# DeltaNet key, value, q and z projections of the second block from high and low parts of h, with beta and dt on four column strips behind the keys

## The reference, cut to what matters

```python
h  = modulate_2(x, norm1_g, sh1, sc1)       # rmsnorm(x) * gain * (1 + scale) + shift
hc = modulate_2(xc, norm1_g, csh1, csc1)    # the same for the context
qkv, z, ba, sc_p, fn_u = split_cols(h @ w_in, IN_SIZES)   # q 512, k 512, v 512, z 512, ba 16, ...
...
qkv = silu(conv_fn(p_qkv, conv_w))          # three taps along the tokens, centred
beta = sigmoid(ba[..., :8])                 # two directions, four heads
g = -exp(a_log) * softplus(ba[..., 8:] + dt_bias)
```

## Time and profile before

| | us |
|---|---|
| three timed runs | 1872.82, 1873.57, 1874.22 (median 1873.57) |
| the profiled execution, its own time | 1871.45 |
| the profiled execution, its span | 1869.6 |
| PE busy | 1780.8 (95% of the span) |
| DVE busy | 913.7 (49%) |
| ACT busy | 614.3 (33%) |
| POOL busy | 125.4 (7%) |
| mean granted TensorE clock | 0.985 |

### The profile page before, as it was taken

One profiled execution on the slowest core, in us unless ns is written; L12 is line 12 of the kernel. 1 busy time (PEld: TensorE's weight loads), 2 busy tenths in 40 slices (PEclk: granted clock), 3 DMA queues, 4 the chain that ended last, 5 costly groups with the idle time before them and its releaser, 6 DMA issues.

```text
span 1869.6 us, 25422 instructions
## 1 busy us (share of the span) xinstructions
PE 1780.8 (95%) x10086; PEld 1337.9 (72%) x10086; DVE 913.7 (49%) x1704; ACT 614.3 (33%) x1155; POOL 125.4 (7%) x138
## 2 busy tenths in 40 slices
PE   6998899999999999898999999999899899999998
PEld 2443445478888887453679999648579799889997
DVE  2133764263434344345736665344468854445554
ACT  3112554142323232133635444302320044034433
POOL 1001000100000001033000000100115000000000
PEclk9999999999999999998999999899999999999999
DMA  9223774322222223244044443313230334344442
GB/s 388 78 90 146 292 278 186 117 104 95 90 91 90 90 91 144 103 156 162 19 156 157 181 181 137 135 61 125 85 135 1 111 132 165 135 150 168 165 155 85
DMA packets 20886, 253.89 MB, mean 136 GB/s; under 512 B 2208, under 2 KB 4512, under 8 KB 5024
## 3 DMA queue, kind: packets, MB, share of 16 engines
q1 hardware_dynamic: 17712, 242.44, 34.2%
q10 hardware_dynamic: 3056, 9.82, 1.4%
HBM read 251.20 MB, written 1.05 MB: 135 GB/s over the span
## 4 chain that ended last, share of the span: by engine, by line
PE 83%; DVE 8%; ACT 3%; DMA 3%; issue 2%; POOL 1%; DVEq 0%; POOLq 0%; SPq 0%; ACTq 0%
PE bank L498 26%; PE bank L524 13%; PE bank L525 13%; PE bank L526 13%; PE bank L924 4%; PE bank L586 3%; PE bank L661 3%; PE bank L684 2%; PE bank L669 2%; DVE w_lo L1582 1%; DMA weights<-in_ada 1%; ACT w_hi L1187 1%; POOL root L2034 1%; ACT slab L1127 1%; DMA weights<-in_even_in 1%
## 5 line engine op out<-in xcount | busy, mean ns | idle before, releaser
L498 PE MATMUL bank<-slab,weights 128*128 128x256 f32 (+2 forms) x1456 | 445.2, 464 | 3.0 <-DVEq L1691 1.2
L498 PEld LDWEIGHTS bank<-slab,weights 128*128 128x128 f32 (+1 forms) x1456 | 272.8, 189 | 169.7 <-issue 134.2
L1582 DVE TENSOR_TENSOR w_lo<-weights,w_hi 128x1024 fp32r<-128x1024 f32 (+1 forms) x220 | 264.4, 1211 | 93.6 <-ACT w_hi L1187 92.7
L1187 ACT ACTIVATE w_hi<-weights 128x1024 fp32r<-128x1024 f32 (+1 forms) x220 | 228.4, 1046 | 215.9 <-PE bank L526 209.6
L524 PE MATMUL bank<-h_hi,w_hi 128*128 128x256 f32 (+1 forms) x864 | 273.9, 317 | 8.5 <-DVE w_lo L1582 5.9
L525 PE MATMUL bank<-h_lo,w_hi 128*128 128x256 f32 (+1 forms) x864 | 273.4, 316 | 0.0
L526 PE MATMUL bank<-h_hi,w_lo 128*128 128x256 f32 (+1 forms) x864 | 272.0, 315 | 0.0
L524 PEld LDWEIGHTS bank<-h_hi,w_hi 128*128 128x128 f32 x864 | 162.9, 189 | 24.9 <-issue 11.4
L525 PE MATMUL bank<-mlp_hidden_lo,w_hi 128*128 128x512 f32 (+1 forms) x512 | 174.4, 341 | 0.0
L524 PE MATMUL bank<-mlp_hidden_hi,w_hi 128*128 128x512 f32 (+1 forms) x512 | 173.3, 338 | 0.6 <-DVE w_lo L1582 0.6
L526 PE MATMUL bank<-mlp_hidden_hi,w_lo 128*128 128x512 f32 (+1 forms) x512 | 172.7, 337 | 0.0
(11 more groups left out here) (209 smaller groups left out, 2305.2 us busy)
## 6 DMA issues: line engine op xcount, KB each, us to landing
weights<-in_ada SPq DMA_DIRECT2D x36, 2048.0 KB, 7.6
weights<-in_mlp_up SPq DMA_DIRECT2D x16, 2048.0 KB, 8.4
weights<-in_mlp_down SPq DMA_DIRECT2D x16, 2048.0 KB, 8.4
weights<-in_ffn_in SPq DMA_DIRECT2D x11, 2048.0 KB, 7.5
weights<-in_in SPq DMA_DIRECT2D x8, 2048.0 KB, 8.5
weights<-in_gate SPq DMA_DIRECT2D x6, 2048.0 KB, 7.6
weights<-in_ffn_out SPq DMA_DIRECT2D x8, 1408.0 KB, 6.0
weights<-in_even_in SPq DMA_DIRECT2D x4, 2048.0 KB, 13.2
```

Of the source, the lines that this page charges most:

```text
L498: last = mm(b[rows, 0:width], lhsT(k), rhs(k), start=k == 0, stop=k == kc - 1)
L1187: A(split_part(w_hi, q), raw_part(q), ACT.Copy).then_inc(sem("w_hi_ready"), 1)
L1582: V.tensor_tensor(split_part(w_lo, q), raw_part(q), split_part(w_hi, q).bitcast(F32), ALU.subtract)\
```

## The change

Keys, values, q and z become `split_linear` layers. Norm 2's second half is written anew: DVE's 16 products go into h, ACT writes their sum with the shift as fp32r into `mix_hi` (16 instructions), DVE writes the low part `mix_lo` (16 instructions, between its products), and ACT then also adds the shift to h in place (16 instructions), since beta and dt, the branches and the gates still read h. PE is released chunk by chunk by `mix2_lo`. ACT and DVE split the first three weight parts ahead of the norm's root.

Beta and dt come behind the four key groups: the 16 weight columns are padded to 32, they are the stationary operand, the 512 tokens move, and the chunks k go to the column strips k % 4, all in one bank. ACT copies the bank to `ba_row`, and behind the first value group four small products add the strips and turn them tokens-first; one DVE copy then takes the place of four. DVE's gate arithmetic stands ahead of its step for v1 and v3, ACT's Sigmoid, Exp and Ln ahead of the Silu of v2.

The splitting of the weights is spread over the groups: ACT splits the high part of group i + 2 ahead of its Silu of group i, DVE the low part of group i + 1 ahead of its wait for group i. The arrays of the layer are placed anew so that `mix_hi` and `mix_lo` fit.

```diff
+            split_linear("in2", [1], tag=lambda m: ("k", m), lead=True, idle=(12, 4),
+                         before=lambda k, m: pe.wait_ge(sem("mix2_lo"), k + 1) if m == 0 else None, **mix_part(TOK))
             w = take_block("in2_ba", 0)
-            for t in range(4):
-                product(("ba", t), DC, lambda k: h[:, k, t * P:(t + 1) * P], lambda k: w[:, k, :], width=16,
-                        before=h_ready("mix2") if t == 0 else None, idle=12 if t == 0 else 0)
-            release_block(("ba", 3))
+            b = open_group(("ba", "strips"))
+            for k in range(DC):
+                pe.wait_ge(sem("mix2_h"), k + 1)
+                strip = slice(k % 4 * STRIP, (k % 4 + 1) * STRIP)
+                ins = mm(b[strip, :], w[:, k, :], h[:, k, :], start=k < 4, stop=k >= 4)
+            close(ins, ("ba", "strips"))
+            release_block(("ba", "strips"))
-            linear("in2", lambda k: h[:, k, :], TOK, tag="k", blocks=[1])
-            linear("in2", lambda k: h[:, k, :], TOK, tag="v", blocks=[2])
-            linear("in2", lambda k: h[:, k, 0:LAT], LAT, tag="q", blocks=[0])
-            linear("in2", lambda k: h[:, k, 0:LAT], LAT, tag="z", blocks=[3])
+            split_linear("in2", [2], tag=lambda m: ("v", m), after=lambda m: gates_tokens_first() if m == 0 else None,
+                         **mix_part(TOK))
+            split_linear("in2", [0], tag=lambda m: ("q", m), **mix_part(LAT))
+            split_linear("in2", [3], tag=lambda m: ("z", m), **mix_part(LAT))
...
+            def gates_tokens_first():
+                b = open_group(("ba", "tokens"))
+                drained(pe, ("ba", "strips"))
+                for t in range(4):
+                    ins = mm(b[:, t * 16:(t + 1) * 16], ba_row[:, t * P:(t + 1) * P], fold[:, 0:16], start=True, stop=True)
+                close(ins, ("ba", "tokens"))
... # scalar engine
-            norm("mix2", TOK, mix2_ready, (2, 0))
+            norm("mix2", TOK, mix2_ready, None, late=PARTS)
+            for c in range(DC):
+                for s in range(SIDES):
+                    act.wait_ge(sem("mix2_m"), c * SIDES + s + 1)
+                    A(mix_hi[:, c, cols], h[:, c, cols], ACT.Identity, bias=mod[2][:, c, s:s + 1])\
+                        .then_inc(sem("mix2_hi"), 1)
+            for c in range(DC):
+                act.wait_ge(sem("mix2_lo"), c + 1)
+                for s in range(SIDES):
+                    ins = A(h[:, c, cols], h[:, c, cols], ACT.Identity, bias=mod[2][:, c, s:s + 1])
+                ins.then_inc(sem("mix2_h"), 1)
+            for i in range(16):
+                split_until(min(parts_before("in2"), PART_END[(name, i % 4)] + PARTS))
+                if i == 4:
+                    copy_out(("ba", "strips"), ba_row)
+                if i == 6:
+                    act.wait_ge(sem("ba_dt"), 1)
+                    ...
... # vector engine
+            split_until(split[0] + PARTS)
             norm_root("mix2", TOK)
-            norm_scale("mix2", TOK, 2, 0)
+            for c in range(DC + 1):
+                if c < DC:
+                    for s in range(SIDES):
+                        V.scalar_tensor_tensor(out=h[:, c, cols], in0=x[:, c, cols], scalar=gains[2][:, c, s:s + 1],
+                                               in1=root[:, 0, cols], op0=ALU.mult, op1=ALU.mult)\
+                            .then_inc(sem("mix2_m"), 1)
+                if c:
+                    for s in range(SIDES):
+                        dve.wait_ge(sem("mix2_hi"), (c - 1) * SIDES + s + 1)
+                        ins = V.scalar_tensor_tensor(out=mix_lo[:, c - 1, cols], in0=h[:, c - 1, cols],
+                                                     scalar=mod[2][:, c - 1, s:s + 1],
+                                                     in1=mix_hi[:, c - 1, cols].bitcast(F32),
+                                                     op0=ALU.add, op1=ALU.subtract)
+                    ins.then_inc(sem("mix2_lo"), 1)
             for i in range(12):
                 t = (name, i % 4)
+                split_until(PART_END[t] + PARTS - 1)
+                if i == 5:
+                    gate_sums()
+                if i == 7:
+                    gate_logs()
                 filled(dve, t)
                 ...
                 conv3(conv[:, i % 3, :], bank(t), taps[:, c + i % 4, :], width, scaled)
+            split_until(parts_before("in2"))
```

More of the change, by code:

```diff
@@ L203, in build @@
         ada_row = root[:, 1, :]
+        ba_row = root[:, 1, :]
         warm = sb("warm", 1)
@@ L512, in linear, with split_linear @@
                     release_block(t)
-            def split_linear(name, blocks, hi, lo, width, tag, before=None, lead=False, idle=(0, 0)):
+            def split_linear(name, blocks, hi, lo, width, tag, before=None, lead=False, after=None, idle=(0, 0)):
                 rows, cols, _ = WEIGHTS[name]
@@ L566, in split_linear @@
                         close(last, t)
+                        if after:
+                            after(m)
                         m += 1
@@ L1115, in norm @@
                     A(dst, x[:, c, 0:width], ACT.Square).then_inc(sem(f"{name}_sq"), 1)
+                split_until(split[0] + late)
                 t = (name, "ss")
@@ L1329, in _ @@
-            for i in range(12):
-                name, dst, width = (("k", kT, TOK), ("v", vT, TOK), ("q", qT, LAT))[i // 4]
-                act.wait_ge(sem("conv"), i + 1)
-                A(dst[:, i % 4, 0:width], conv[:, i % 3, 0:width], ACT.Silu).then_inc(sem(f"{name}_silu"), 1)
-            for i in range(4):
-                filled(act, ("z", i))
-                A(zs[:, i, :], bank(("z", i))[:, 0:LAT], ACT.Silu).then_inc(free(("z", i)), 1)
+            norm("mix2", TOK, mix2_ready, None, late=PARTS)
@@ new lines, in gate_sums @@
+            def gate_sums():
+                t = ("ba", "tokens")
+                filled(dve, t)
+                V.tensor_copy(gsum, bank(t)[:, 0:64].rearrange("p (t c) -> p t c", c=16)).then_inc(free(t), 1)
+                drained(dve, t)
+                for t in range(4):
+                    link(V.tensor_tensor(dtmp[:, 0, t, :], gsum[:, t, 8:16], par("dt_bias"), ALU.add))
+                link(V.tensor_scalar(dtmp[:, 2], dtmp[:, 0], -1.0, None, ALU.mult))
+                link(V.tensor_tensor(dtmp[:, 1], dtmp[:, 0], dtmp[:, 2], ALU.max))
+                V.tensor_scalar(dtmp[:, 0], dtmp[:, 0], 0.0, None, ALU.max).then_inc(sem("ba_dt"), 1)
@@ new lines, in gate_logs @@
+            def gate_logs():
+                dve.wait_ge(sem("ba_dt"), 1)
+                dve.wait_ge(sem("gate_parts"), 3)
+                link(V.tensor_tensor(dtmp[:, 0], dtmp[:, 0], dtmp[:, 2], ALU.add))
+                for t in range(4):
+                    link(V.scalar_tensor_tensor(out=gl[:, t, :], in0=dtmp[:, 0, t, :], scalar=-1.0,
+                                                in1=decay[:, 0:8], op0=ALU.mult, op1=ALU.mult))
+                V.engine_nop().then_inc(sem("g_ready"), 1)
```

73 lines of the change are left out of this document (37 added, 36 removed).

## The result

The kernel after takes 1853.29 us (median of 4 runs, 1850.75 to 1860.84) against 1873.89 us for the kernel before on the same chip (4 runs, 1872.82 to 1877.64): ratio 0.9893, 95% interval 0.9880 to 0.9907. The forecast was 1853.2 in a range of 1847 to 1861. The profiled execution took 1854.92 us, with a span of 1853.0.

What follows compares the result with a forecast made beforehand. PE was taken to bound the projections. Terms summed to 79.3 us, with the clock's 1.7 to 81.0 against 101.3, 20.3 less: median 1853.2 us from 1873.57, range 1847 to 1861 for 8 in 10.

Steps and rivals of the forecast that it cites:

- Groups: Sixteen key, value, q and z groups: 82.6 us before, 67.8 in three passes, 14.7 less; 512-wide groups 5.60, 256-wide 2.88.
- rival (c): Projections: three passes cost three quarters of four when fed without a break, 61.9 us for 67.8; 1847.3, chance 0.06.
- (a): DVE stays behind after the fourth-key-group wait; eight value and q groups cost 1.3 us more each; 1863.5, chance 0.15.
- (d): Slower: each value and q group's low part waits for the step of the group just closed; 1884, chance 0.04.
- 1.4 us of slack: Each value group: DVE has 4.2 us of work against PE's 5.60, so low parts stay ahead.
- Start and three key groups: Keys start 2.74 us behind DVE's first product, at 1185.97; first three key groups take 16.87, ending at 1202.84.
- The gap: Before the fourth key group PE waits 4.8 us for DVE's low part, made behind two steps; bounds 2.2 and 6.5.
- ACT is just as late: At the fourth key group: ACT's high part is ready at 1206.0, near DVE's low part with hand-over at 1207.6.
- The clock in the gap: PE idles about 2.9 us before the fourth key group, the clock falls, 1.7 us lost; bounds nothing and twice that.
- Strips and small products: Beta and dt: eight strip products 1.9 us, four small products 0.95, at most twice that; ACT's table loads covered.
- Passage to q: From values to q PE waits 1.7 us, then 0.4 twice, for DVE's steps and low parts: 2.5 us, bounds 0 and 5.
- Rival (e): Projections' gain given back: l2 stage or delta net waits for a weight block; nothing left, 1873, chance 0.03.

Runs made afterwards that it cites:

- the experiments at the fourth group and at q: Kernel after with the fourth key group's parts made earlier, 1849.24 us; that kernel with weight parts one group further ahead from the last value group on, 1846.28 us.

## Why the prediction was right

By its own steps, from DVE's first product on.

**Groups.** DVE's steps for the values:

```profile
1221.03 0.75 DVE L1825 TENSOR_SCALAR slab<-bank,params 128x512 f32<-128x512 f32 x1 [3.48 <-PE bank L529]
...
1227.54 0.75 DVE L1825 TENSOR_SCALAR slab<-bank,params 128x512 f32<-128x512 f32 x1 [0.75 <-PE bank L529]
...
1233.14 0.75 DVE L1825 TENSOR_SCALAR slab<-bank,params 128x512 f32<-128x512 f32 x1 [1.44 <-PE bank L529]
...
1238.74 0.75 DVE L1825 TENSOR_SCALAR slab<-bank,params 128x512 f32<-128x512 f32 x1 [0.53 <-PE bank L529]
```

They are 5.60 apart, 6.51 where the small products lie, so rival (c) falls here as in the rows of before, and DVE waits ahead of each, so rivals (a) and (d) fall too. The forecast's 1.4 us of slack is there ahead of the third value step (1.44); where the gates' small instructions stand, ahead of the second and the fourth, 0.75 and 0.53 are left. So (a) had a true ground that was too small to matter here.

**Start and three key groups.** The keys start 2.73 us behind DVE's product (forecast 2.74) and the three groups take 1184.57 to 1201.45, 16.88 (16.87). The parts split ahead of the root cost nothing that shows.

**The gap.** 1201.45 to 1206.03, 4.58 (4.8), ended by DVE's low part, in the order that the forecast had:

```profile
1198.86 0.75 DVE L1825 TENSOR_SCALAR slab<-bank,params 128x512 f32<-128x512 f32 x1 [3.27 <-PE bank L529]
...
1201.73 0.75 DVE L1825 TENSOR_SCALAR slab<-bank,params 128x512 f32<-128x512 f32 x1
...
1204.66 1.22 DVE L1621 TENSOR_TENSOR w_lo<-weights,w_hi 128x1024 fp32r<-128x1024 f32 x1
```

"ACT is just as late" was wrong; it had its high part 1.1 us before DVE took it up:

```profile
1200.73 1.28 ACT L1374 ACT_TABLE_LOAD   x1
1202.02 0.63 ACT L1374 ACTIVATE slab<-slab 128x512 f32<-128x512 f32 x1
1202.56 1.04 ACT L1209 ACTIVATE w_hi<-weights 128x1024 fp32r<-128x1024 f32 x1
```

The Silu starts 0.01 us behind the load, so no row has room for a second piece, and leaving it out was right. The drain of about 1.38 us that the Trainium skill (ScalarE: Activation LUTs, What ACT_TABLE_LOAD costs) adds to a load is not borne out here.

**The clock in the gap.** 3.4 us at 0.51, so 1.7 lost, as taken. That it fell here was not certain: behind the same gap it fell in three of five profiles. The forecast had "nothing" as its other bound.

**Strips and small products.** 1.92 and, by the second value step, 6.51 - 5.60 = 0.91 (1.9 and 0.95). The gates' table loads lay under a value group.

**Passage to q.** From the last value step, at 1238.74, to the turn of v 25.3 us for eight groups of 2.88: 2.3 lost, 1.5 of them in the one wait at the second q group (2.5).

**Sum.** 20.3 us less was forecast for the stage and 20.6 measured. The bounds of its terms, added up, give 1846.4 to 1860.1 and not the 1848 to 1858 that it states; the range of 1847 to 1861 covers all but 0.6 us of that.

Rival (e), the gain given back downstream, came true in part in the profiled run, 5.3 us, but not as it was put: no weight block was waited for. One of the prediction's own signs of being wrong, a longer stage from the l2 norms on, did appear (220.57 against 215.25). For an execution like the profiled one it forecast 1851.1, and the profiled run of after took 1854.92, 3.8 more. The prediction had no term for half clock that comes and goes from run to run, though it makes up most of the range that the runs span. That the median fell within 0.1 us of the forecast is partly luck for this reason.

What the prediction did not see, as it priced only the sum: that one half of the change, made first, is worth three times the other in the stage, 15.7 to 4.9. The passes' gross gain of 14.7 was right. The gap with its clock (6.3), the passage to q (2.3) and the later start (1.3) took 9.9 of it back, and the experiments at the fourth group and at q recovered 6.8 of that.

## What to carry to other kernels

Price the two halves of a change apart, also where they come together: here the cheap one, moving small products off the head of a stage and giving them 512 columns, carries three quarters of the stage's gain when made first, and its time alone can't be told from that of the whole change. A faster product hands the bound to whoever prepares its operands: look for the first group whose preparation stands behind a consumer's step in the same queue, and move it ahead. And before a few us are explained, take the half-clock time out of the runs: time x clock tells kernels apart that their times do not.

## What the runs showed of the hardware

Products 16 columns wide ran with TensorE at 1.2 GHz at two places of the program. Behind the keys the clock fell 2.9 us into them, at 1222.2, though PE had been busy since 1213.60, and stayed at 0.50 over the next 8.00 us. Ahead of the keys it fell while PE was still waiting for ACT's shifts (busy 2.08 of 4.10 us), and stayed low while the products ran without a break (0.63 on the mean of the gates, rows 2). Eight products on strips with 512 columns had no such stretch behind them in the kernel with the gates alone moved. Time lost to half clock is most of what one run of a kernel differs by from the next: 30 to 43 us of 1871 to 1885 in the kernel before. An idle time of 2.69 us behind dummies was followed by 3.4 us at half clock in three profiles of five. Three passes with high and low parts cost 0.82 of true f32 at 512 columns (5.60 to 6.87) and 0.83 at 256 (2.88 to 3.45) at the full clock.
